# Two token halves accumulated side by side, over two pairs of PSUM banks, in output projection and feed-forward

## What is computed

```python
merged = g_sb * o_sb.reshape(B, L, W_Q) + g_fx * o_fx.reshape(B, L, W_Q)
x = x + jnp.einsum('blm,md->bld', merged, w_o)
h = _rms_norm(x, g_ffn)
u = jnp.square(jax.nn.relu(jnp.einsum('bld,df->blf', h, w_up)))
return x + jnp.einsum('blf,fd->bld', u, w_down)
```

## Time and profile before

| | |
|---|---|
| median of the runs | 3726.23 us |
| runs | 3726.23, 3727.31, 3721.62 us |
| span of the profiled execution (first to last instruction) | 3723.1 us |
| what lies between that span and the median | 3.1 us |
| mean granted TensorE clock | 0.989 |
| busy: TensorE, VectorE, ScalarE, GpSimd | 3579.6, 1644.7, 1359.4, 342.7 us |
| HBM traffic over the span | 115 GB/s |

### The profile page before, as it was taken

One profiled execution on the slowest core, in us unless ns is written; L12 is line 12 of the kernel. 1 busy time (PEld: TensorE's weight loads), 2 busy tenths in 40 slices (PEclk: granted clock), 3 DMA queues, 4 the chain that ended last, 5 costly groups with the idle time before them and its releaser, 6 DMA issues.

```text
span 3723.1 us, 71770 instructions
## 1 busy us (share of the span) xinstructions
PE 3579.6 (96%) x26809; PEld 3414.6 (92%) x26809; DVE 1644.7 (44%) x2307; ACT 1359.4 (37%) x1917; POOL 342.7 (9%) x625
## 2 busy tenths in 40 slices
PE   6999999999999998998989989999999999999999
PEld 5999999999999987877779979999999999999998
DVE  3225666664444446666772243333333333333333
ACT  3224555554444444556651132222222221212121
POOL 0111111111111112222320000000000000000000
PEclk8999999999999999999999999999999999999999
DMA  4433333333332327667993222322232223223322
GB/s 151 115 108 96 84 95 94 89 81 91 88 98 83 96 58 236 219 212 250 319 329 101 79 57 91 89 90 81 90 89 88 82 90 88 89 82 90 89 87 84
DMA packets 480624, 430.75 MB, mean 116 GB/s; under 512 B 22145, under 2 KB 420354, under 8 KB 479250
## 3 DMA queue, kind: packets, MB, share of 16 engines
q1 hardware_dynamic: 441426, 311.74, 28.8%
q0 software_dynamic: 39136, 118.17, 9.6%
HBM read 405.95 MB, written 23.89 MB: 115 GB/s over the span
## 4 chain that ended last, share of the span: by engine, by line
PE 86%; DVE 6%; issue 4%; ACT 3%; DMA 1%; SPq 0%; ACTq 0%; DVEq 0%; POOL 0%; POOLq 0%
PE ps L603 27%; PE ps L604 26%; PE ps L605 26%; PE ps L813 3%; PE ps L738 1%; DVE E L1459 1%; DVE E L1453 1%; PE ps L644 1%; DVE n_t L1357 1%; DVE Z L1462 1%; PE ps L654 0%; PE ps L718 0%; PE ps L717 0%; ACT E L1129 0%; ACT E L1127 0%
## 5 line engine op out<-in xcount | busy, mean ns | idle before, releaser
L603 PE MATMUL ps<-h_hi,w_hi 128*128 128x268 f32 x2592 | 764.2, 295 | 13.2 <-DVE h_lo L1330 10.3
L603 PE MATMUL ps<-m_hi,w_hi 128*128 128x268 f32 x2560 | 735.8, 287 | 28.5 <-DVE m_lo L1330 11.0
L605 PE MATMUL ps<-h_lo,w_hi 128*128 128x268 f32 x2592 | 744.9, 287 | 0.0
L604 PE MATMUL ps<-h_hi,w_lo 128*128 128x268 f32 x2592 | 743.9, 287 | 0.0
L605 PE MATMUL ps<-m_lo,w_hi 128*128 128x268 f32 x2560 | 735.0, 287 | 0.0
L604 PE MATMUL ps<-m_hi,w_lo 128*128 128x268 f32 x2560 | 733.3, 286 | 0.0
L1005 ACT ACTIVATE w_hi<-w_raw 128x2048 fp32r<-128x2048 f32 x225 | 429.7, 1910 | 772.9 <-PE ps L605 762.0
L1330 DVE TENSOR_TENSOR w_lo<-w_raw,w_hi 128x2048 fp32r<-128x2048 f32 x225 | 515.4, 2291 | 356.7 <-ACT w_hi L1005 353.7
L603 PE MATMUL ps<-u_hi,w_hi 128*128 128x268 f32 x2048 | 584.3, 285 | 5.7 <-ACT r_sb L1287 5.7
L604 PE MATMUL ps<-u_hi,w_lo 128*128 128x268 f32 x2048 | 587.0, 287 | 0.0
L605 PE MATMUL ps<-u_lo,w_hi 128*128 128x268 f32 x2048 | 586.8, 287 | 0.0
(11 more groups left out here) (255 smaller groups left out, 4501.0 us busy)
## 6 DMA issues: line engine op xcount, KB each, us to landing
w_raw<-in_w_in_dram SPq DMA_DIRECT2D x81, 1024.0 KB, 5.9
w_raw<-in_w_up_dram SPq DMA_DIRECT2D x64, 1024.0 KB, 6.3
w_raw<-in_w_down_dram SPq DMA_DIRECT2D x64, 1024.0 KB, 5.4
w_raw<-in_w_out_dram SPq DMA_DIRECT2D x16, 1024.0 KB, 5.8
kraw<-kT_dram POOLq DMA_DIRECT2D x32, 264.0 KB, 3.1
mg_dram<-mg POOLq DMA_DIRECT2D x32, 264.0 KB, 2.3
vraw<-out_dram POOLq DMA_DIRECT2D x32, 256.0 KB, 3.3
pg<-in_cache_sb_k_dram SPq DMA_DIRECT2D x32, 256.0 KB, 3.0
```

What stands on the lines that cost most here:

```text
L603: pe.matmul(out, whi, xhi, start=first, stop=False)
L604: pe.matmul(out, wlo, xhi, start=False, stop=False)
L605: return pe.matmul(out, whi, xlo, start=False, stop=last)
```

## The change

In `wout`, `up` and `down` the two halves of the tokens no longer follow one another. For each block, TensorE multiplies both halves by the high weights (high activations, then low activations: four matmuls with the same weights), then both by the low weights. The two halves fill a pair of banks; pairs 0 (banks 0, 1) and 1 (banks 2, 3) take turns from slab to slab, in `down` from `t` to `t`. `dense_ok` rises by 2 at the end of the pair, and ScalarE and VectorE wait for the whole pair. TensorE waits for a free pair, not a free bank. The first down product of a chunk waits for `u_lo` of both halves. The projections ahead of attention keep `dense`.

```diff
+            def both_halves(pair, wh, wl, xh, xl, ks, first, last):
+                banks = [ps[:, B_DENSE + 2 * pair + half, 0:HT] for half in range(2)]
+                cols = [slice(half * HT, (half + 1) * HT) for half in range(2)]
+                for k in ks:
+                    for half in range(2):
+                        pe.matmul(banks[half], wh(k), xh[:, k, cols[half]], start=(k == first), stop=False)
+                    for half in range(2):
+                        pe.matmul(banks[half], wh(k), xl[:, k, cols[half]], start=False, stop=False)
+                    for half in range(2):
+                        mm = pe.matmul(banks[half], wl(k), xh[:, k, cols[half]], start=False, stop=(k == last))
+                if ks[-1] == last:
+                    mm.then_inc(dense_ok, 2)
+            def slab_halves(s, pair, hi, lo, ks=range(KT)):
+                both_halves(pair, lambda k: w_hi[s.slot][:, k, :], lambda k: w_lo[s.slot][:, k, :], hi, lo, ks, 0, KT - 1)
...
-                    for half in range(2):
-                        dense(s, half, m_hi, m_lo, evac_v, s.banks + (half - 2 * S_WO - 1 + FREE_DENSE))
+                    pe.wait_ge(w_lo_ok, s.number + 1)
+                    pe.wait_ge(evac_v, s.banks + (-2 * S_WO - 2 + FREE_DENSE))
+                    slab_halves(s, s.slot, m_hi, m_lo)
...
+                    pe.wait_ge(w_lo_ok, s.number + 1)
+                    pe.wait_ge(evac_a, c * 16 + j * 4 + (2 * S_WO + 2 * u - 2 + FREE_DENSE))
+                    if not normed:
+                        slab_halves(s, s.slot, m_hi, m_lo)
+                        return
...
-                        for half in range(2):
-                            if t == 0 and u == 0 and isinstance(j, int):
-                                pe.wait_ge(u_lo_ok, c * 16 + (15 + half + U0))
-                            pe.wait_ge(evac_v, c * 32 + j * 8 + (32 + 4 * u + 2 * t + half - 1 + FREE_DENSE))
...
+                        if t == 0 and u == 0 and isinstance(j, int):
+                            pe.wait_ge(u_lo_ok, c * 16 + (16 + U0))
+                        pe.wait_ge(evac_v, c * 32 + j * 8 + (32 + 4 * u + 2 * t - 2 + FREE_DENSE))
+                        both_halves(t, lambda k: wh[:, k, t * P:(t + 1) * P], lambda k: wl[:, k, t * P:(t + 1) * P],
+                                    u_hi, u_lo, range(8), 0, 7)
...
-                    act.wait_ge(dense_ok, s.banks + (half + 1 + DENSE0))
-                    act.activation(r_sb[u][:, cols], ps[:, B_DENSE + half, 0:HT], ACT.Relu).then_inc(evac_a, 1)
+                    act.wait_ge(dense_ok, s.banks + (2 + DENSE0))
+                    act.activation(r_sb[u][:, cols], ps[:, B_DENSE + 2 * s.slot + half, 0:HT], ACT.Relu).then_inc(evac_a, 1)
...
-                dve.wait_ge(dense_ok, s.banks + (k + 1 + DENSE0))
+                dve.wait_ge(dense_ok, s.banks + (2 * (k // 2) + 2 + DENSE0))
...
-                dve.tensor_tensor(v, v, ps[:, B_DENSE + half, 0:HT], ALU.add).then_inc(evac_v, 1)
+                dve.tensor_tensor(v, v, ps[:, B_DENSE + 2 * pair + half, 0:HT], ALU.add).then_inc(evac_v, 1)
```

More of the change, by code:

```diff
@@ L904, in _ @@
             pe.matmul(ps[:, B_O + 1, 0:P], ones[:, :], diag[:, :], start=True, stop=True).then_inc(self_ps, 1)
+            def both_halves(pair, wh, wl, xh, xl, ks, first, last):
[12 more added lines that the diff above has]
+                both_halves(pair, lambda k: w_hi[s.slot][:, k, :], lambda k: w_lo[s.slot][:, k, :], hi, lo, ks, 0, KT - 1)
             def wout(s, first=False):
                 if not first:
-                    for half in range(2):
-                        dense(s, half, m_hi, m_lo, evac_v, s.banks + (half - 2 * S_WO - 1 + FREE_DENSE))
+                    pe.wait_ge(w_lo_ok, s.number + 1)
+                    pe.wait_ge(evac_v, s.banks + (-2 * S_WO - 2 + FREE_DENSE))
+                    slab_halves(s, s.slot, m_hi, m_lo)
                     return
                 pe.wait_ge(evac_a, 2 * S_WO + FREE_DENSE)
+                pe.wait_ge(w_lo_ok, s.number + 1)
                 for q in range(4):
                     pe.wait_ge(m_lo_ok, q + 1)
-                    for half in range(2):
-                        dense(s, half, m_hi, m_lo, evac_v, half - 1 + FREE_DENSE, (4 * q, 4 * q + 4))
+                    slab_halves(s, s.slot, m_hi, m_lo, range(4 * q, 4 * q + 4))
             wout(Slab(S_WO), True)
@@ L931, in up @@
                 def up(u, j, normed=False):
[L932 to L938, removed]
+                    s = up_slab(u, c, j)
+                    pe.wait_ge(w_lo_ok, s.number + 1)
+                    pe.wait_ge(evac_a, c * 16 + j * 4 + (2 * S_WO + 2 * u - 2 + FREE_DENSE))
+                    if not normed:
+                        slab_halves(s, s.slot, m_hi, m_lo)
+                        return
+                    for k in range(0, KT, 2):
+                        pe.wait_ge(nrm[1]["lo"], k + 2)
+                        slab_halves(s, s.slot, m_hi, m_lo, range(k, k + 2))
                 if first:
@@ L1677, in _, with add_bank @@
             dve.wait_ge(x_ld, 16)
-            def add_bank(s, half, m, k):
-                dve.wait_ge(dense_ok, s.banks + (k + 1 + DENSE0))
+            def add_bank(s, half, m, k, pair):
+                dve.wait_ge(dense_ok, s.banks + (2 * (k // 2) + 2 + DENSE0))
                 v = x2T[:, m, half * HT:(half + 1) * HT] if isinstance(m, int) else \
                     x2T[:, bass.ds(m, 1), half * HT:(half + 1) * HT].rearrange("p o t -> p (o t)")
-                dve.tensor_tensor(v, v, ps[:, B_DENSE + half, 0:HT], ALU.add).then_inc(evac_v, 1)
+                dve.tensor_tensor(v, v, ps[:, B_DENSE + 2 * pair + half, 0:HT], ALU.add).then_inc(evac_v, 1)
             def wout(s, nxt, m):
@@ L1688, in wout @@
                 for half in range(2):
-                    add_bank(s, half, m, half)
+                    add_bank(s, half, m, half, s.slot)
             wout(Slab(S_WO), Slab(S_WO + 1), 0)
@@ L1717, in down @@
                     for half in range(2):
-                        add_bank(s, half, j * 4 + (2 * u + t), 2 * t + half)
+                        add_bank(s, half, j * 4 + (2 * u + t), 2 * t + half, t)
             def ffn(c, final):
```

## The result

The changed kernel takes 3769.67 us (median of 4 runs, 3768.76 to 3775.15) against 3723.93 us for the kernel before in the same session (3720.90 to 3727.31). The ratio is 1.0121, 95% interval 1.0106 to 1.0135: 45.7 us slower, between 39 and 50. The forecast was 3768 us, 41.8 us slower.

A forecast was written before the change was run, and what follows sets the result against it. TensorE, 96% busy, was taken as the bound: only matmul pitch and its stops could move time. 0 + 26.7 + 11.2 + 3.9 = 41.8 us on 3723.1 gave 3764.9, plus 3.1 to the runs' median: 3768 us, range 3735 to 3795.

The forecast's parts named there:

- Step 1: Output projection and feed-forward matmuls: using the same weights four times saves no load time, 0 us.
- Step 2: Turn from up to down, 8 times: both halves' ScalarE/VectorE chain is exposed, 3.34 us more each, 26.7 us.
- No other matmul is ready: Claim at the up-to-down turn that nothing covers the exposed chain, 26.7 us over 8 turns.
- Step 3: After each of 8 up-to-down stops the granted clock falls to 0.50, 1.4 us lost each, 11.2 us.
- the 5.62 us row: Earlier low-clock stretch after 2.93 us idle; as upper end, half of it lost at each up-to-down turn, 22.4 us.
- Step 4: Turns from `w_out` to norm, down to up, and the end: one more 0.43 us addition exposed, 9 times, 3.9 us.
- What costs nothing: Waits for a free pair and later weight splits in the slabs stay covered, 4.5 us to spare; no cost.
- The faster rival: Load spared at 9,216 matmuls with repeated weights, 10.6 ns each, 98 us in all: 3670 us; chance 0.12.
- The clock stays up: Rival: after the up-to-down stops the clock does not fall, 11 us less: 3757 us; chance 0.2.
- the third rival: Clock falls at down-to-up turns too (10 us more), or for longer (11 more): 3778 to 3789 us; chance 0.08.

The follow-up runs named there:

- the version with the spare pair: Changed kernel with the free bank pair filled first at both turns and later waits, the last u awaited only before block 7; 3709.20 us, ratio 0.9954.
- the last run: The version with the spare pair, but each slab runs half 0 whole before half 1; 3709.43 us, ratio 0.9952 against the kernel before.
- the run that has the weights in turn: Changed kernel, halves still side by side, but high and low weights alternating, so 1 of 6 matmuls repeats weights instead of 4; 3771.68 us, ratio 1.0122.
- the filled stop: Changed kernel with 31 products into an unread bank ahead of the wait at each up-to-down turn; 3755.58 us, ratio 1.0078.

## Why the prediction was right, step by step

**Step 1 (0 us).** Right. 123.9 ns per matmul with the weights repeated, 124.0 with them in turn, and equal numbers of loads and matmuls. The 16-column products of the earlier trace rows were the decisive rows: there the load alone was visible, and repeated weights did not shorten it. The load records that the prediction speaks of are these, with the same `sel` ahead of L718 and other weights ahead of L717 (shortest, median and longest in ns):

```profile
L717 PEld LDWEIGHTS ps<-nck_hi,sel x96: 187/188/192, 838.3 to 1376.2; 128*128 128x128 f32 x96
L718 PEld LDWEIGHTS ps<-nck_lo,sel x96: 187/188/192, 838.4 to 1376.3; 128*128 128x128 f32 x96
```

The 7 ns that one group of the earlier trace rows had at 384 columns would have misled; at 268 columns nothing of it appeared. The bank that changes with every matmul costs nothing that the runs resolve: it does so in the version with the spare pair, but not in the last run, which is as fast. Their two windows give 123.5 and 123.3 ns per matmul; on 13,824 matmuls that would be under 3 us.

**Step 2 (26.7 us).** Right, 1 to 2 us too high: idle time at these turns grew by 30.8 - 5.7 = 25.1 us, and the runs leave 26. The chain is the one written out. Most of the surplus is in the last hand-over: the prediction used 0.32 us, the delay from a Relu to TensorE, and the trace shows 0.12 us from VectorE's low part to TensorE (2470.46 to 2470.58). "No other matmul is ready" holds only for where the change puts its wait: the version with the spare pair finds 42 products of blocks 0 to 6 that are.

**Step 3 (11.2 us).** The mechanism was right and its size too low: 14 to 16 us by the experiment that removes it, 16.5 us of missing work in the profiled execution, which was the longest of its four. The prediction gave every turn the 2.99 us stretch of the earlier trace rows, 1.4 us lost. In that execution three turns have a short one (44 matmuls in 7 us, 1.6 us lost) and five a long one (37 to 39, 2.2 to 2.5 us lost), more like the 5.62 us row that had been kept as the upper end. At chunk 1 the clock fell not right behind the stop, as the prediction had it, but 0.8 us later (rows at the end of this document).

**Step 4 (3.9 us).** Right in kind, a little high where the trace measures it: the 7 turns from down to up cost 10.0 - 7.5 = 2.5 us more, since the two additions of a pair run into one another (0.78 us for both instead of twice 0.43). The run with only the up-to-down turn undone lies 2.8 us above the kernel before. The clock did not fall at these turns. One of them in the changed kernel, the two additions and then the 7 us behind it:

```profile
2567.41 0.78 DVE L1699 TENSOR_TENSOR x2T<-x2T,ps 128x268 f32<-128x268 f32 x2 [5.16 <-PE ps L917]
2568.78:2575.78 7.00, 7.00 (x56) 1.00 0.29 80
```

At the turn from `w_out` to the norm the term is not resolved: from the first product of `w_out` to that of the feed-forward stage it is 0.3 us more (239.02 instead of 238.75, from the rows above).

**What costs nothing.** Right. TensorE never waits for `w_lo` between slabs; the only stops in the feed-forward stage are those of the two turns.

The sum was 41.8 us. The steps measured give 0, then 25 to 26, 14 to 16.5 and 3, together 42 to 45.5; the medians differ by 45.7, with an interval of 39 to 50. That forecast and median lie within 2 us of each other is partly luck: Step 3 was 3 to 5 us too low and Step 2 up to 2 too high, and with its fourth run the median of the kernel before fell by 2.3 us. The faster rival (the load spared) fell with the run that has the weights in turn. "The clock stays up" fell with the windows behind the 8 stops, and the filled stop gave its price. Of the third rival, the clock did stay low for longer at five turns, but it did not fall at the turns from down to up.

## What to carry to other kernels

Interleaving two accumulations makes them end together, and then whatever the first one used to hide at the next dependency is bare: write the chain out in program order and look for what else is ready to run. Before counting on reused weights, find the narrowest matmuls in the trace whose weights repeat; they show the load's own price. When a second set of banks is there, its worth lies at the turns of the loop: start the next stage in the free set, with the operands that are ready, and place the wait in front of the one that is not.

## What was not expected of the hardware

A stop of 2.2 us among dense matmuls lowered the clock at 3 of 8 turns of one execution, under the same program and the same stop; after about 4 us it fell at 8 of 8. And the low stretch behind equal stops comes in two lengths: three turns of the changed kernel lost 13 of 57 matmuls in 7 us, five lost 18 to 20; in its twin with the weights in turn six were short and two long. At a short one of the changed kernel (chunk 1) TensorE first ran 6 products at the full clock, and then it fell; at a long one (chunk 3) the first products were already slow:

```profile
2470.58:2471.38 0.80, 0.80 (x6) 1.00 0.00 0
2471.40:2474.60 3.20, 3.20 (x17) 0.50 0.03 5
...
2865.28:2866.10 0.82, 0.81 (x3) 0.50 0.00 0
```

So a clock read only at the first product behind a stop would have missed the loss at chunk 1. TensorE was dense on both sides of every one of these stops; why the clock fell earlier at some turns than at others is not shown.
